# A mixture-of-experts layer: expert outputs scattered by token instead of gathered by slot

## What is computed

```
expert = g_idx * EXPERTS_PER_GROUP + e_idx            # two per token
...
xb = x[slot_tok].reshape(n_blocks, MOE_BLOCK, D)      # tokens sorted by expert
def expert_block(args):
    xs, e = args
    gate, up = jnp.split(xs @ w_e_in[e], 2, axis=-1)  # 1024 x 1024
    return (jax.nn.silu(gate) * up) @ w_e_out[e]      # 512 x 1024
yb = lax.map(expert_block, (xb, block_exp)).reshape(n_slots, D)
y = jnp.zeros((NT, D), f32).at[slot_tok].add(yb.astype(f32) * slot_w[:, None])
```

## Time and profile before

| what | value |
|---|---|
| time, median of 3 runs | 1780.25 us (1778.27 to 1783.7) |
| the profiled execution's own time | 1780.19 us |
| its span, first to last instruction | 1778.4 us |
| mean granted TensorE clock, share of full | 0.979 |
| HBM read, written | 316.42 MB, 58.74 MB |

### The profile page before, as it was taken

One profiled execution on the slowest core, in us unless ns is written; L12 is line 12 of the kernel. 1 busy time (PEld: TensorE's weight loads), 2 busy tenths in 40 slices (PEclk: granted clock), 3 DMA queues, 4 the chain that ended last, 5 costly groups with the idle time before them and its releaser, 6 DMA issues.

```text
span 1778.4 us, 35422 instructions
## 1 busy us (share of the span) xinstructions
PE 1670.4 (94%) x14793; PEld 930.9 (52%) x14793; DVE 1012.6 (57%) x2453; ACT 442.4 (25%) x1072; POOL 211.8 (12%) x311
## 2 busy tenths in 40 slices
PE   5999999999999999999999999987999999999990
PEld 3455444544444545555455545545777775555550
DVE  2486526555555354443544435555778877776754
ACT  5120324333444212222122121112222122122110
POOL 3030000000110222202222051010000000000003
PEclk9999999999999999999999999988999999999995
DMA  9377218001211110101101176489899999999997
GB/s 350 120 265 252 71 71 263 25 24 32 63 48 52 47 33 16 33 21 31 34 16 33 56 292 232 148 284 370 330 425 427 426 427 426 429 427 427 429 422 303
DMA packets 109014, 363.70 MB, mean 205 GB/s; under 512 B 12890, under 2 KB 56840, under 8 KB 96428
## 3 DMA queue, kind: packets, MB, share of 16 engines
q1 hardware_dynamic: 86256, 282.70, 41.0%
q10 hardware_dynamic: 15708, 54.73, 8.4%
q0 software_dynamic: 6960, 25.04, 3.8%
HBM read 316.42 MB, written 58.74 MB: 211 GB/s over the span
## 4 chain that ended last, share of the span: by engine, by line
PE 80%; DMA 14%; DVE 3%; POOL 1%; issue 1%; ACT 1%; SPq 1%; ACTq 0%; POOLq 0%; DVEq 0%
PE bank L298 78%; DMA arena<-in_w_e_out 11%; DMA arena<-in_w_in 1%; POOL arena L759 1%; PE bank L945 1%; DMA arena<-y_slots,ints 1%; SPq L380 1%; DVE arena L2396 0%; DVE arena L1887 0%; PE bank L1233 0%; ACTq L1397 0%; DMA arena<-in_kn_g_c 0%; DVE arena L2386 0%; ACT arena L1523 0%; DMA x_slots<-arena,ints 0%
## 5 line engine op out<-in xcount | busy, mean ns | idle before, releaser
L298 PE MATMUL bank<-arena 128*32 128x256 f32 (+7 forms) x14414 | 1627.4, 388 | 36.4 <-DMA arena<-in_w_e_in 7.1
L298 PEld LDWEIGHTS bank<-arena 128*32 128x32 f32 (+3 forms) x14414 | 884.7, 131 | 748.5 <-issue 548.1
L2386 DVE STREAM_TRANSPOSE arena<-arena 32x256 f32<-32x256 f32 x372 | 161.9, 435 | 5.7
L2396 DVE STREAM_TRANSPOSE arena<-arena 32x128 f32<-32x128 f32 x384 | 157.5, 410 | 4.8
L1725 ACT ACTIVATE arena<-bank 128x128 f32<-128x128 f32 x96 | 19.7, 278 | 395.4 <-PE bank L298 395.4
L1717 ACT ACTIVATE arena<-arena 128x96 f32<-128x96 f32 x248 | 92.1, 460 | 5.2 <-DVE arena L2386 5.2
L2377 DVE TENSOR_TENSOR arena<-bank,arena 128x512 f32<-128x512 f32 x64 | 35.5, 557 | 99.9 <-PE bank L298 99.8
L2144 DVE TENSOR_TENSOR arena<-arena,bank 128x128 f32<-128x128 f32 (+1 forms) x40 | 11.4, 286 | 130.3 <-PE bank L298 130.3
L759 POOL DMA_INDIRECT arena<-y_slots,ints x16 | 17.1, 1070 | 542.9 <-DMA y_slots<-arena 537.9
L684 POOL TENSOR_TENSOR arena<-arena 64x256 f32<-64x256 f32 x96 | 70.2, 731 | 30.3 <-DVE arena L2120 23.7
L1887 DVE RECIPROCAL arena<-arena 128x512 f32<-128x512 f32 x10 | 33.5, 3349 | 30.8 <-ACT arena L1452 30.8
(11 more groups left out here) (337 smaller groups left out, 1030.1 us busy)
## 6 DMA issues: line engine op xcount, KB each, us to landing
arena<-in_w_e_in SPq DMA_DIRECT2D x64, 2048.0 KB, 24.4
arena<-in_w_e_out SPq DMA_DIRECT2D x32, 2048.0 KB, 25.2
arena<-in_w_ada SPq DMA_DIRECT2D x12, 2048.0 KB, 12.4
arena<-in_w_in SPq DMA_DIRECT2D x32, 512.0 KB, 3.8
arena<-x_slots ACTq DMA_DIRECT2D x32, 512.0 KB, 10.3
y_slots<-arena ACTq DMA_DIRECT2D x32, 288.0 KB, 9.3
y_slots<-arena POOLq DMA_DIRECT2D x21, 384.0 KB, 17.2
arena<-in_w_in SPq DMA_DIRECT2D x3, 2048.0 KB, 21.3
```

What stands on the lines that cost most here:

```text
L298: return nc.tensor.matmul(o, l, r, start=start, stop=stop)
L2386: ins = V.transpose(e_xT[s][ts(b, QT), :, ts(t, QT)], rows[:, :, b, :])
L2396: ins = V.transpose(hT[ts(q, QT), :, ts(t, QT)], e_h[ts(c, QT), r, :].rearrange("p (n k) -> p k n", k=4))
```

## The change

The expert's result rows are no longer stored by slot. POOL scatters them by indirect DMA straight to the rows of their tokens in a DRAM tensor `y_rows` of 2 x 1024 rows: first choices in rows 0 to 1023, second choices in 1024 to 2047. The list of target rows, one column of 96 numbers for each expert (`i_row`), is made behind the router: DVE writes for each tile two one-hot tables, `r_hot` (which rank has this token) and `r_in` (which expert, times the token's target row minus 2048), 16 matmuls sum their products in a PSUM bank, and DVE adds 2048 and rounds to integers. A slot without a token gets the number 2048, which lies outside of `y_rows`; the DMA drops such a row.

What moves or goes with it: the 21 zero fills and the waits on them are gone; ACT's queue has no stores of y; `y_out` puts the 256 columns that stand in partitions 96 to 127 back beside the other 768, with three more operations over 32 partitions x 256 columns, so that a row is 4096 bytes in one partition. In the final sums SP loads `y_rows` with eight plain DMAs of 1024 KB (both rows of 128 tokens), each tile into buffers of its own, at most four under way. Buffers: the last expert's `e_hTl`, the second `e_y` and `r_hot` lie over constants of the mixer. The extra blocks' code is changed alike and isn't run here.

```diff
@@ final loads, on SP
+            sp.wait_ge(sem("extra_end"), 1)
+            for a in range(2):
+                sp.wait_ge(sem(f"y_st{a}"), 16 * NE // 2)
+            for t in range(NT):
+                if t >= 4:
+                    sp.wait_ge(fy_in[t % 4][0], fy_in[t % 4][1] + 16)
+                sp.dma_start(f_y[t], y_t[t]).then_inc(fy_in[t % 4][0], 16)
@@ POOL
-            pool.wait_ge(sem("proj"), 8)
-            for b in range(NE, NB):
-                pool.dma_start(ys_b[b].rearrange("p (a n) -> p a n", a=8), KC[0:CAP, 0:P].unsqueeze(1).to_broadcast([CAP, 8, P]))\
-                    .then_inc(sem("slots_zero"), 16)
...
+            def scatter(y, ix, stored):
+                pool.sem_inc(sem("gather_go"), 1)
+                pool.indirect_dma_start(out=ytok_d, out_offset=bass.IndirectOffsetOnAxis(ap=ix[0:CAP], axis=0), in_=y[0:CAP, :],
+                                        in_offset=None, bounds_check=TOPK * T - 1, oob_is_err=False).then_inc(stored, 16)
+
+            def scatter_of(e, s, stored):
+                if stored is not None:
+                    pool.wait_ge(sem(f"y_st{s}"), stored)
+                G.tensor_copy(i_rx[s], i_row[:, ds(e, 1)]).then_inc(sem("rx_set"), 1)
+                pool.wait_ge(sem("rx_set"), e + 1)
+                pool.wait_ge(sem("y_out"), 2 * e + 2)
+                scatter(e_y[s], i_rx[s], sem(f"y_st{s}"))
+
+            pool.wait_ge(sem("router_dve"), TABLE)
+            scatter_of(0, 0, None)
+            scatter_of(1, 1, None)
+            with pool.Fori(1, NE // 2) as i:
+                for s in range(2):
+                    scatter_of(2 * i + s, s, 16 * i)
...
-            for t in range(NT):
-                if t >= 4:
-                    pool.wait_ge(sem("f_sum"), t - 3)
-                for k, ix in enumerate((i_s1, i_s2)):
-                    pool.indirect_dma_start(out=f_y[t % 4][k], out_offset=None, in_=yslot_d,
-                                            in_offset=bass.IndirectOffsetOnAxis(ap=ix[:, t:t + 1], axis=0))\
-                        .then_inc(fy_in[t % 4][0], 16)
@@ PE
             pe.wait_ge(sem("router_dve"), COUNTS)
+            for n in range(NT * TOPK):
+                ins = mm(PS[7][:, 0:NE], r_hot[:, n // TOPK, n % TOPK], r_in[:, n // TOPK, n % TOPK], n == 0, n == NT * TOPK - 1)
+            ins.then_inc(sem("r_mm"), 1)
...
             xT(0, 0)
+            pe.wait_ge(sem("router_dve"), TABLE)
@@ ACT
-            def store_rows(b, y, stored):
-
-                rows = ys_b[ds(b, 1)].rearrange("o p n -> (o p) n")
-                act.dma_start(rows[0:CAP, 0:768], y[0:CAP, :]).then_inc(stored, 16)
-                act.dma_start(rows[0:CAP, 768:D].rearrange("(t p) n -> p t n", p=QT),
-                              y[CAP:P, :].rearrange("p (t n) -> p t n", t=3)).then_inc(stored, 16)
@@ DVE, place(t)
+                TT(r_in[:, t], r_m[:, t], bc(r_tok[:, t], NE), ALU.mult)
+                TT(r_hot[:, t], r_iP.unsqueeze(1).to_broadcast([P, TOPK, P]), bc(r_rank[:, t], P), ALU.is_equal)
@@ DVE, behind the last weights of the router
+            dve.wait_ge(sem("r_mm"), NT + 1)
+            TS(i_row, PS[7][:, 0:NE], float(2 * T), None, ALU.add).then_inc(sem("router_dve"), 1)
@@ DVE, y_out
-                    TT(e_y[s][:, cols], PS[5 + u][:, 0:(512, 256)[u]], gt2[:, cols], ALU.mult).then_inc(sem("y_out"), 1)
+                    for r in ((0, 1), (2,))[u]:
+                        TT(e_y[s][ts(r, QT), 768:D], PS[5 + u][CAP:P, ts(r % 2, 256)], gt2[CAP:P, ts(r, 256)], ALU.mult)
+                    TT(e_y[s][0:CAP, cols], PS[5 + u][0:CAP, 0:(512, 256)[u]], gt2[0:CAP, cols], ALU.mult).then_inc(sem("y_out"), 1)
```

More of the change, by code:

```diff
@@ L98, in hybrid_block @@
         ident, ones = small(P), small(P)
+        e_y1 = view(at[0], D)
         msk = small(4, P)
@@ L272, in hybrid_block @@
         sb_i = ctx.enter_context(nc.sbuf_tensor("ints", [P, 160], i32))[:, :]
-        i_tok, i_s1, i_s2 = (sb_i[:, 8 * k:8 * k + 8] for k in range(3))
+        i_tok, i_row, i_rowx = sb_i[:, 0:8], sb_i[:, 8:8 + NE], sb_i[:, 122:122 + NX]
+        i_rx = [sb_i[:, 144 + k:145 + k] for k in range(3)]
         i_tab = sb_i[:, 40:40 + NBP]
@@ L290, in hybrid_block @@
         f_x = [view(12288 + 1024 * t, D) for t in range(NT)]
-        f_y = [[view(2048 * i, D), view(2048 * i + 1024, D)] for i in range(4)]
+        f_y = [view(2048 * t if t < 6 else 20480 + 2048 * (t - 6), TOPK, D) for t in range(NT)]
         def bc(ap, n):
@@ L745, in _ @@
                             .then_inc(sem("extra_xs"), 16)
+                        pool.wait_ge(sem("y_out"), 2 * (NE + j) + 2)
+                        scatter(e_y[0], i_rx[2], sem("y_stx"))
+                        pool.wait_ge(sem("y_stx"), 16 * j + 16)
                     with pool.Else():
@@ L1748, in _ @@
             load_x(4, 0)
-            store(0, 0)
             silu(2)
@@ L1752, in _ @@
             load_x(5, 1)
-            store(1, 1)
             silu(3)
@@ L1756, in _ @@
             load_x(6, 0)
-            store(2, 0)
             def pair(e, ahead=2):
@@ L1763, in pair @@
                     load_x(e + 3, 1)
-                store(e - 1, 1)
                 silu(e + 1)
@@ L2417, in _ @@
             activate(3)
-            y_out(2, 0, 32)
+            y_out(2, 0, 16)
             turn_h(3)
@@ L2423, in pair @@
                 activate(e)
-                y_out(e - 1, 1, 32 * (i - 1))
+                y_out(e - 1, 1, 16 * (i - 1))
                 turn_h(e)
@@ L2427, in pair @@
                 activate(e + 1)
-                y_out(e, 0, 32 * i)
+                y_out(e, 0, 16 * i)
                 turn_h(e + 1)
```

62 lines of the change are left out of this document (26 added, 36 removed).

## The result

The changed kernel takes 1786.8 us (median of 22 runs, 1783.1 to 1788.2), the kernel before 1783.2 on the same chip (median of 22). The ratio is 1.0021, interval 1.0014 to 1.0027: 0.2% slower, 3.7 us. That is inside the 0.3% that I had called no change, with the sign opposite to my -1.3 us and above my range, 1769.5 to 1783.5.

The account below looks back on a forecast made before the run. The prediction took the DMA engines' work between about 1290 and 1690 us to bound the expert stage. Scatter -0.8 and end -0.5 made -1.3 us on 1780.2, so 1778.9 us, range 1769.5 to 1783.5.

Parts of the forecast that it names:

- "so it costs nothing" for VectorE in the stage: Expert stage: three added copies per expert, 1.27 us, fall where PE runs ahead of the weights; 0 us, 1 without cover.
- "0" behind the router: After the router: index table matmuls and PE's wait end before the first x rows land; covered by 4 us, cost 0.
- "+1.3 us" for the copies ahead of the last `second`: Kernel's end: `y_out` of expert 30 is on the chain before the last `second` and PE waits for it; +1.3 us.
- The -0.8 of the scatter: Expert stage: rows dealt in blocks of six, busiest engine 1.00 us against 1.03 an expert; -0.8 us over 24 experts.
- the base: Time of the kernel before on which the sum stood: its profiled execution, 1780.2 us, with run median 1780.25.
- What bounds the kernel: Expert stage: full DMA engines from about 1290 to 1690 us set its end, 16.87 us an expert against PE's 15.54.
- Rival 1: Expert stage: scattered rows dealt to engines in turn, so saved bytes count; -8 us there, 1771.7 us in all; chance 0.36.
- Rival 2: Expert stage: four neighbouring rows per engine give eight engines 8 full rows; +7.2 us, 1786.9 us; chance 0.08.
- rival 3: Expert stage: a scattered row costs more under load, 0.194 us; +3.1 us, up to 1784 with a bad end; chance 0.06.
- Rival 4: Scatter: dropped rows are written elsewhere, so traffic is not saved; time as the forecast, and its chance counted there.
- The rest of the end: After the last `second`: one operation +0.4, scatter landing +1.2, SP's start -0.7, plain loads instead of gathers -2.7 us.
- The zero fills, 0: Stretch from 110 to 150 us: removing the fills saves nothing, since matmuls there wait for no DMA; 0 us.

Follow-up runs that it names:

- dealt: Changed kernel with an expert's slots renumbered by additional VectorE operations so full rows spread over the engines; ratio to the kernel before 1.0040, stage 449.30 us.
- no_drop: Changed kernel with nothing dropped, each empty slot's row written to a row of its own behind `y_rows`; ratio to the kernel before 1.0025.
- no_small: Changed kernel without the three 32x256 copies of `y_out`, so those output columns are wrong; ratio to the kernel before 0.9992.
- act_quarter: Changed kernel with the three 32x256 copies moved to ScalarE and the gate applied in the final sums; ratio to the kernel before 1.0009.
- act_mm: `act_quarter` plus 14 small matmuls that move a 16 KB instruction load out of the last scatter; ratio to the kernel before 1.0000.
- before_shifted: Kernel before with 64 empty TensorE instructions that left nothing in the built program, so a repeat of it; ratio 1.0009.

## Why the prediction was wrong

Three steps failed: "so it costs nothing" for VectorE in the stage (measured +0.9 us), "0" behind the router (+0.9 to 1.8) and "+1.3 us" for the copies ahead of the last `second` (+2.9). The -0.8 of the scatter measured 0, and the base was 3.0 us too low.

**What bounds the kernel: right.** The pace of 16.8 us and the full DMA engines stayed, and `dealt` and `no_drop` agree with the account by the busiest engine.

**The scatter in blocks, -0.8: right in kind, not seen in size.** b without copies is 454.28 to 454.35 with the scatter (`no_small`, `act_quarter`, `act_mm`) and 453.78 to 454.45 without, so 6 rows scattered cost what 6 rows stored cost, and -0.8 measured 0. Rival 1 had its mechanism wrong and its price about right (I had 8 us, `dealt` shows 5.9). Rival 2 (more than six rows on an engine, in groups of four) would have shown intervals of 17.15 throughout; most are 16.82 to 16.87, which rules out rival 3 too. Rival 4 didn't occur, no bytes were moved for dropped rows, and `no_drop` shows that it would have had no effect, as said.

**VectorE "so it costs nothing": wrong in the stage.** The stall at the block count grew from 17.06 to 17.86 us, as forecast, and PE started its stalls on weights one expert later, so that this stall was covered, as forecast. But at the block owners, near 1600, PE no longer runs ahead; there the copies cost 0.9 us that nothing gives back. I had looked at one of the three places where VectorE has block sums to do, and at that one for which there is cover.

**The end, "+1.3 us" for the copies ahead of the last `second`: the mechanism right, the size wrong.** This term and the two that stood at nothing, VectorE in the stage and the part behind the router, put the sum on the wrong side. c grew by 2.9 us, not 1.3. I added the copies' time to the chain and left the matmuls behind them at 7.07 us, their length in the earlier trace rows, in which the lower clock was already contained. In `before_shifted`, the same program, they take 5.39 us, and with the copies 1.3 to 1.7 us more in nine of eleven profiles. (Against the one profile on which the sum stood the term did come: c grew from 40.45 to 41.70, by 1.25 us. It fails against the kernel's usual execution, and so against the median.) One profile of before couldn't tell that; but its had 96 matmuls of the same kind at 5.43 us, and I did not set the two beside each other. The rest of the end came as said: 5.5 us to SP's first load (5.4), 29.9 to the last sum (29.4), so d fell by 1.6 us where the terms of the forecast give 1.8.

**Behind the router, 0: a cost that the sum left out, 0.9 to 1.8 us.** Each step that I named was covered, "table and wait" too. What was missing is no step of the work: the matmuls shift the program, so that a load of instructions falls into a scatter on which the first expert waits.

**The zero fills, 0: right.** The 336 matmuls that run on the chain from 133 us on take 110.51 us in both profiles.

With the measured terms the sum is 0 (scatter) + 0.9 + 2.9 + 1.8 - 1.6 = +4.0 us on 1783.2. Of the 7.9 us between 1778.9 and 1786.8 the base is 3.0; the rest is 1.7 in the stage (+0.9 for -0.8), 1.6 in c and 0.9 to 1.8 behind the router. The change stayed within 0.3%, to which I had given 0.53, but that is in part luck: three terms came out too low, none by more than 2 us. The range was too narrow, since it hung on a base from three runs.

## What to carry to other kernels

Before a saving of bytes is counted, ask how the transfer is dealt to the engines: rows left out of a block of consecutive ones save nothing while another block stays full. Work that moves to an engine is covered only where that engine has slack in every turn of the loop, so look at the turns with extra work and at the last one, and cost a longer wait of TensorE with the clock of the matmuls behind it. Look for loads of instructions, for large loads and for stores of single elements beside each scatter or gather that something waits for. And take a second profile of the kernel before: one execution can already contain the loss that the change would bring.

## What the runs showed of the hardware

- An indirect DMA of 96 rows of 4 KB goes to the 16 DMA engines in blocks of six consecutive rows; a dropped row moves no bytes. In the last expert's scatter 35 dropped rows leave 35 packets of 4 bytes, all within 0.12 us (1746.885 to 1747.0 us). The 61 full rows are ten blocks of six and one row, so five engines would have nothing but dropped rows, 30 of the 35; and 29 of them are done by 1746.97, before any full row can have ended (the first starts at 1746.82 and takes 0.16 us):

```profile
DMA packets 42, 0.03 MB, mean 251 GB/s; under 512 B 35, under 2 KB 35, under 8 KB 42
```

- TensorE's 16 KB loads of instructions (14 matmuls more moved one from 1205.84 to 1200.43) take 0.9 to 1.7 us of one DMA engine, and delay the landing of a 1 MB scatter by 0.9 to 1.8 us.
- A scatter to `x_slots` lands after 3.5 us alone (the last tile of the kernel before) and 6.2 to 6.4 us beside a load of x of 0.5 MB; 2048 stores of 4 bytes from SyncE's queue stretched it to 14.25 us, a load of 2 MB without them to 10.03.
- The 32x32 transposes of VectorE over 256 columns cost 435 ns with neighbouring output columns and 637 ns with every sixth.
- A load of 96 rows in place of 128 made the 2 MB weight loads beside it dearer by 8.5% (2.54 us a MB for 2.34); not explained.
